# Eight modulation sums moved from the output projection to the first MLP matrix

## The reference, cut to what matters

```python
cond = jax.nn.silu(c)
mod = (cond @ ada_w[l] + ada_b[l]).reshape(B, 6, D_MODEL)[:, :, None, :]
shift2, scale2, gate2 = mod[:, 3], mod[:, 4], mod[:, 5]
...
x = x + gate1 * (merged @ w_o[l])
u2 = rmsnorm(x, norm_mlp[l]) * (1.0 + scale2) + shift2
h = jnp.square(jax.nn.relu(u2 @ w_ff1[l]))
x = x + gate2 * (h @ w_ff2[l])
```

## Time and profile before

| what | value |
|---|---|
| median of 3 runs | 984.34 us (982.01 to 984.48) |
| span of the profiled execution | 980.8 us |
| TensorE busy in it | 934.8 us, 95% |
| GpSimd busy | 739.2 us, 75% |
| VectorE busy | 665.4 us, 68% |
| ScalarE busy | 492.7 us, 50% |

### The profile page before, as it was taken

One profiled execution on the slowest core, in us unless ns is written; L12 is line 12 of the kernel. 1 busy time (PEld: TensorE's weight loads), 2 busy tenths in 40 slices (PEclk: granted clock), 3 DMA queues, 4 the chain that ended last, 5 costly groups with the idle time before them and its releaser, 6 DMA issues.

```text
span 980.8 us, 21945 instructions
## 1 busy us (share of the span) xinstructions
PE 934.8 (95%) x7758; PEld 909.3 (93%) x7758; DVE 665.4 (68%) x1097; ACT 492.7 (50%) x811; POOL 739.2 (75%) x894
## 2 busy tenths in 40 slices
PE   6999899999789999999999999999989999999996
PEld 6898789999779999999899999999988999999996
DVE  4979996765877774652566678886466666888722
ACT  3455556654346665554454455444454444544441
POOL 1486565677687999998677659999956676799973
PEclk9999999999999999999999999999999999999999
DMA  9985555646453557565354444555515444455521
GB/s 374 401 321 178 212 177 210 236 152 246 164 192 130 204 190 273 179 216 209 129 172 155 150 166 172 174 192 194 211 45 178 167 171 155 146 192 194 178 101 43
DMA packets 28222, 185.20 MB, mean 189 GB/s; under 512 B 3027, under 2 KB 5504, under 8 KB 6272
## 3 DMA queue, kind: packets, MB, share of 16 engines
q1 hardware_dynamic: 25832, 167.93, 47.5%
q10 hardware_dynamic: 2328, 16.40, 4.6%
HBM read 183.26 MB, written 1.07 MB: 188 GB/s over the span
## 4 chain that ended last, share of the span: by engine, by line
PE 74%; DVE 16%; issue 5%; ACT 3%; DMA 1%; DVEq 1%; POOL 0%; SPq 0%; POOLq 0%; ACTq 0%
PE mm L544 21%; PE mm L545 21%; PE mm L546 21%; ACT w_hi L1001 1%; PE mm L578 1%; DVE cy L1967 1%; DVE w_lo L1406 1%; PE mm L562 1%; DVE cy L1972 1%; PE ps_s L871 1%; DVE qr L1991 1%; PE ps_o L888 1%; PE ps_o L962 1%; DVE rt L1990 1%; DVE mix_lo L1936 1%
## 5 line engine op out<-in xcount | busy, mean ns | idle before, releaser
L470 POOL TENSOR_TENSOR w_lo<-raw,w_hi 128x256 fp32r<-128x256 f32 x876 | 729.7, 869 | 215.4 <-ACT w_hi L1001 212.9
L544 PE MATMUL mm<-u_hi,w_hi 128*128 128x256 f32 x1616 | 462.2, 286 | 4.6 <-issue 4.4
L545 PE MATMUL mm<-u_lo,w_hi 128*128 128x256 f32 x1616 | 449.5, 278 | 0.0
L546 PE MATMUL mm<-u_hi,w_lo 128*128 128x256 f32 x1616 | 449.4, 278 | 0.0
L1001 ACT ACTIVATE w_hi<-raw 128x1024 fp32r<-128x1024 f32 x291 | 306.2, 1058 | 144.1 <-PE mm L546 139.6
L544 PEld LDWEIGHTS mm<-u_hi,w_hi 128*128 128x128 f32 x1616 | 304.9, 189 | 12.4 <-issue 11.9
L545 PEld LDWEIGHTS mm<-u_lo,w_hi 128*128 128x128 f32 x1616 | 304.0, 188 | 2.0 <-issue 1.9
L546 PEld LDWEIGHTS mm<-u_hi,w_lo 128*128 128x128 f32 x1616 | 304.4, 188 | 0.0
L1406 DVE TENSOR_TENSOR w_lo<-raw,w_hi 128x1024 fp32r<-128x1024 f32 x72 | 103.4, 1436 | 58.0 <-ACT w_hi L1001 55.4
L544 PE MATMUL mm<-mix_hi,w_hi 128*128 128x256 f32 x256 | 71.7, 280 | 1.5 <-DVE mix_lo L1976 1.5
L545 PE MATMUL mm<-mix_lo,w_hi 128*128 128x256 f32 x256 | 71.4, 279 | 0.0
(11 more groups left out here) (292 smaller groups left out, 1331.1 us busy)
## 6 DMA issues: line engine op xcount, KB each, us to landing
raw<-weights SPq DMA_DIRECT2D x145, 1024.0 KB, 4.8
ada_raw<-ada ACTq DMA_DIRECT2D x14, 1024.0 KB, 5.3
ada_raw<-ada SPq DMA_DIRECT2D x6, 1024.0 KB, 12.4
ada_more<-ada SPq DMA_DIRECT2D x4, 1024.0 KB, 12.7
bias<-tab_scratch SPq DMA_DIRECT2D x1, 1536.0 KB, 9.3
dec<-decay ACTq DMA_DIRECT2D x1, 1536.0 KB, 8.8
x<-xT SPq DMA_DIRECT2D x1, 1024.0 KB, 9.9
out<-x SPq DMA_DIRECT2D x4, 256.0 KB, 2.3
```

The costliest lines, as they stand in the source:

```text
L470: ins = nc.gpsimd.tensor_tensor(w_lo[:, s, at], r[:, at], hi[:, at], ALU.subtract)
L544: nc.tensor.matmul(dst, wh, rhs_hi(k), start=a, stop=False)
L545: nc.tensor.matmul(dst, wh, rhs_lo(k), start=False, stop=False)
L546: i = nc.tensor.matmul(dst, wl, rhs_hi(k), start=False, stop=b)
```

## The change

It takes the eight steps out of WO (and from behind the making of `u`) and puts each behind one unit of F1, units 2, 4, 6, 8, 14, 16, 20 and 22, after that unit's `h_lo` and, where VectorE has one there, its `w_lo`. The loads of the pairs 22 and 23 move from WO units 2 and 4 to F1 units 7 and 10, on the same queue of ScalarE. So that the steps can stand at uneven places, VectorE's part of F1 is written out in full, and ScalarE's for its first 16 units.

```diff
+    GATE2_AT = [2, 4, 6, 8, 14, 16, 20, 22]
+    GATE2_LOAD = {7: 22, 10: 23}
...
@@ scalar, output projection
             high(None, U_WO + j + SLOTS)
-            if j in (2, 4):
-                ada_load(act, 21 + j // 2)
             act.wait_ge(taken[o % 4], o // 4 + 1)
             square_x(1, j, x[:, j, :])
@@ scalar, up_turn
                 A(dst, relu_h[:, f % 2, :], ACT.Square).then_inc(S["hh_ready"], 1)
-
-        up_turn(None, 0)
-        with act.Fori(0, 3) as g:
-            up_turn(g, 8)
+                if g is None and f in GATE2_LOAD:
+                    ada_load(act, GATE2_LOAD[f])
+
+        for base in (0, 8):
+            up_turn(None, base)
+        with act.Fori(0, 2) as g:
+            up_turn(g, 16)
@@ vector, output projection
             if j:
                 add_square(1, j - 1)
-            if j < KC - 1:
-                ada_step(5 * KC + j)
         variance(1)
         dve.wait_ge(S["rstd_ready"], 2)
         make_u(1, lambda k: a_mix[:, 1, k:k + 1], SHIFT2)
-
-        ada_step(6 * KC - 1)
@@ vector, up_turn
                 low(g, c + SLOTS)
-
-        up_turn(None, 0)
-        with dve.Fori(0, 3) as g:
-            own.enter(g, 8)
-            up_turn(g, 8)
-            own.leave(3)
+                if f in GATE2_AT:
+                    ada_step(5 * KC + GATE2_AT.index(f))
+
+        for base in range(0, 32, 8):
+            up_turn(None, base)
```

## The result

| | before | changed |
|---|---|---|
| median | 984.41 us (20 runs, 981.22 to 995.34) | 993.73 us (20 runs, 987.91 to 1001.29) |
| ratio | 1 | 1.0092, 95% interval 1.0068 to 1.0117 |
| span of the profiled execution | 980.8 us | 992.6 us |

The changed kernel is slower by 9.3 us in the medians, where 4.6 was forecast; by the interval it is 6.7 to 11.5 us. With 12 more runs of it in a second session (e4) it is 3.3 to 10.2. In some executions TensorE runs a stretch of 13.7 or 17.1 us between the two layers at 1.2 GHz. The five traces that have it have a mean granted clock of 0.984 to 0.986, the others 0.991 to 0.995. Parted by that clock at 0.99, 35 runs of before and 32 of the changed kernel fall in two groups each. In the group of the higher clock the change costs 8.1 us (means of 983.4 and 991.5), in the other 6.3 (991.7 and 997.9), or 7.2 if two runs at 0.989 are counted to the first.

A forecast was written before the change was run, and what follows sets the result against it. The prediction took TensorE as the bound overall, with GpSimd equally full in F1 and becoming its bound after the change. WO's -3.1 and F1's +7.7 us summed to +4.6, from 984.34 to 988.9 us, range 985.0 to 991.0.

The forecast's parts named there:

- GpSimd as the bound of F1, 1.0 us a step: F1: eight steps each lengthen a GpSimd operation by 1.0 us, less 0.3 reserve: +7.7 us, bounds 0 and 9.9.
- the one of 1 us at unit 90: F1: a TensorE wait of about 1 us at unit 90, among the signs that the forecast is right.
- -3.1 forecast: WO: without seven steps TensorE's waits at units 65 and 66 go, 3.1 us gained, bounds 2.6 and 3.6.
- Loads, queues, code, VectorE's reserve: WO and F1: moved loads, queues and written-out code cost 0, bounds -0.3 and +0.7; VectorE's fuller turns cause no wait.
- The thin place at f = 4: F1, VectorE's tightest place: ScalarE wants `h_lo` after 8.8 us against 10.2, so no wait, but thin.
- Rival C: F1: part of the steps meet GpSimd cheaply, 0.7 us a step, F1 loses 5.3, total 986.5 us; chance 0.20.
- Rival E: F1: waits up to 2.6 us might lower TensorE's clock; changes the sum by 0.5 at most, no chance of its own.
- TensorE runs on at its old pace: F1: after each wait for GpSimd TensorE runs at its old pace, 2.72 us a unit, so nothing is won back.
- F2 as it was: F2: stays unchanged, among the signs that the forecast is right.
- A changed F2: F2: a change there was listed as a sign of a wrong forecast, beside GpSimd idle in F1 and others' waits.
- the sum of 4.6: Whole kernel: -3.1 us in WO plus 7.7 in F1 gives +4.6 us, 984.34 to 988.9.

The follow-up runs named there:

- e4: The changed kernel, unaltered, run again in a second session for a second trace and more times: 994.24 us, ratio 1.0069 (1.0033 to 1.0104).
- e2: Kernel before, steps left in WO, their condition row copied to PSUM by ScalarE: 984.96 us, 0.9988 of before; timed again 987.66 us, 0.9997.
- e15: The kernel before, unaltered, run again for a third trace: 991.6 us.
- e7: The kernel before with one spare 128x128 matmul between F1 and F2: 983.49 us, timed once.
- e11: The changed kernel with two spare 128x128 matmuls between F1 and F2: 992.20 us, 1.0051 of before (1.0024 to 1.0078).
- e10: The changed kernel with the steps' condition row in PSUM and each step done twice; no whole time given, F1 83.43 us, F2 90.87 us.
- e5: The changed kernel with the steps' condition row in PSUM, plus one spare 128x128 matmul between F1 and F2: 990.04 us, timed once.
- e13: Kernel before with the steps' condition row in PSUM, steps in WO, plus 27 spare matmuls through the program: 983.98 us, ratio 0.9991 (0.9963 to 1.002).

## Why the prediction was right and wrong

**GpSimd as the bound of F1, 1.0 us a step: right.** F1 takes 89.9 to 90.6 us in the four traces of the changed kernel and 82.3 in two of before: 7.6 to 8.3 more, against 7.7 forecast. Against the third of before (84.9) it is 5.0 to 5.7 more. The waits stand at units 74, 78, 86 and 94; the one of 1 us at unit 90 didn't come, its loss arrived with that of 94 (1.5 and 0.25 just ahead). That the cause is the operand in SBUF, and not VectorE's time or queue, is shown by the row in PSUM, which takes the waits of the steps away at either place (0.4 us stay in F1, where before has 0.57), and by the half steps.

The Trainium skill ("SBUF — State Buffer", Who interferes with whom) says that a VectorE instruction with at most one SBUF input, outside the modes that use two ports, doesn't contend with GpSimd. The trace of e2 agrees: 0.74 us for each of GpSimd's operations beside the step. The Trainium skill ("SBUF — State Buffer", Terms) also calls the lock exclusive and held for a full instruction. The traces agree with this too, more closely than the prediction had it: both engines wait in turn, and the price is 1.0 and not 1.28 us, since a step that came while an operation ran ended 1.08 us after that one, not 1.28.

**WO: right.** -3.1 forecast; -2.7 to -3.2 in the four traces of the changed kernel, -3.1 without the steps at all, all against the first trace of before. In the third (e15) WO took 21.85 us with one wait, so the gain isn't the same in each execution.

**Loads, queues, code, VectorE's reserve: right.** The norm moved by 0.1 us, no wait in F1 was for a load, and VectorE with twice the steps held up ScalarE (14.0 us) but not TensorE. The thin place at f = 4 held; the prediction's sum for it, 8.8 us, should be 7.1 + 1.3 = 8.4, which leaves the verdict as it was.

**Rival C: no.** The waits of F1 add up to 7.9, 7.0, 6.4 and 6.2 us in the four traces, so they vary by the 1 to 2 us of which it spoke; but where they are short, TensorE was the slower between them, and F1 itself stays within 0.7 us.

**Rival E: right in what it said.** Waits of 2.2, 2.0 and 1.9 us in F1 left the granted clock at 1.00 in the window of that stage.

**"TensorE runs on at its old pace" and "F2 as it was": wrong, and this is the step that failed.** A changed F2 was the prediction's own sign of being wrong. The unit of 2.72 us, 24 matmuls at 113.3 ns, was read from one trace of before and taken for the kernel's. It is one of two, 2.72 or 2.83 us, and what a stream gets was different from one execution to the next. F2 took 87.04 us in two traces of the changed kernel and 90.44 in the other two; of the three traces of before it was 90.44 in one. From the start of unit 60 to the end of F2, before takes 206.1, 206.1 and 212.1 us, and 206.3 with a spare matmul (e7), mean 207.6; the changed kernel 215.1, 210.9, 211.5 and 214.6, and 211.9 with two (e11), mean 212.8. Traces of like pace in F2 differ by 5.3 us in the faster, near the sum of 4.6, and by 2.8 in the slower, of which before has one trace; that TensorE's own turn, there 11.3 us, hides more of GpSimd's would account for it, but was not tried by itself. The profiled pair, 11.8 us apart, is an unlike one: 3.4 us of it are F2's pace. Over the whole program 446 us of the changed kernel's trace ran in the slower pace against 276 of before's; at 3.8% that is an estimated 6.5 of the 11.8 us, which the prediction put at nothing.

**What stays open.** The medians lie 9.3 us apart and the groups 8.1 and 6.3, and the traces show 5.2 in this stretch; 1 to 4 us aren't placed, since behind F2 the traces of the two kernels (506.5 to 508.4 and 506.3 to 508.3 us to the last matmul, but for those with the stretch at 1.2 GHz) don't differ. The pace explains the one profiled pair, but the traces don't show that the changed kernel draws the slower oftener: over the whole program it had it for 446, 346, 296 and 394 us, mean 370, and the three traces of before for 276, 318 and 548, mean 381. So why the medians are 9.3 us apart and not about 5 stays open. That the pace makes up the rest is a guess that these means don't support. What decides the pace behind a wait isn't known either.

## What to carry to other kernels

An engine that is full beside TensorE has a price list for its neighbour's operations; read it from the one operation that is longer than its fellows, and move such work only to where that engine waits anyway, or move one operand to PSUM, where here GpSimd was not held up. Before a stage is taken "as it was", divide its matmuls by its time in two or three traces of the same kernel: a stage that is 100% busy at full clock may still be 4% longer in the next execution. And what a trace shows as gained by 3 us of 984 need not show in the time; here it didn't, at 0.9988 and 0.9997.

## What the runs showed of the hardware that was not expected

- In F1 and F2 the stream of 128x256 matmuls started one every 113.3 or 117.8 ns (118.3 in F2 of e10), at a granted clock of 1.00 in both; the slower made up 276 and 548 us of two traces of the kernel of before.
- A break of 0.15 us, by one small matmul, was enough for the stream to come back in the other pace (e5). After such breaks it was the faster 11 times of 11, after waits for data 19 of 34.
- VectorE operations and GpSimd's `w_lo`, all with two inputs in SBUF, took turns: in F1 a step of 1024 columns ended 1.08 us (0.55 with 512 columns) after the GpSimd operation under way, and GpSimd's next 0.60 after the step. That lengthens one GpSimd operation by 1.0 or 0.45 us, and the step from 1.28 to 1.76. With one input in PSUM neither happens (e2).
- Three traces (e2, e4, e5) have 17.1 us at 1.2 GHz between the layers, two (e11, e13) 13.7. Of the runs, 15 of 35 of before and 16 of 32 of the changed kernel have the low mean clock that goes with it, and take 8.3 and 6.5 us longer; half of 17.1, the clock's own share if TensorE were busy throughout, is 8.5.
